# Two attention stages rearranged: search, sums and division in one, the latent heads moved to the other

## The chip, the cores and the metric

The program runs on one core of one Trainium2 chip. It computes one mixture-of-experts block and two layers of a second network on 1024 tokens of width 1024, all in fp32. The metric is the device time of one execution in microseconds (us), lower is better.

## The reference, cut to what matters

Three kinds of dense attention are touched: the latent heads of the first block, and in each of the two layers of the second block the "map" heads and the "grouped" heads. All are a plain softmax over all keys:

```python
# first block, latent heads: 8 heads, q and k of 96 (64 + 32 rotary), v of 64, 1024 queries, 1024 keys
s = jnp.einsum('bqhd,bkhd->bhqk', q_blk, k).astype(jnp.float32) * scale
p = jax.nn.softmax(s, axis=-1).astype(v.dtype)
return jnp.einsum('bhqk,bkhd->bqhd', p, v)

# second block, two layers: 1024 + 256 context keys
# map heads: 4 heads x 2 maps = 8 softmaxes of width 32, v of 64
s = jnp.einsum('bqhmd,bkhmd->bhmqk', q, k).astype(jnp.float32) * (q.shape[-1] ** -0.5)
p = jax.nn.softmax(s, axis=-1)
a = (p[:, :, 0] - lam * p[:, :, 1]).astype(v.dtype)
# grouped heads: 6 query heads of 64 on 2 key heads
```

Layer 0 of the second block also attends from the 256 context queries to the 256 context keys. Layer 1 does not need them.

## The kernel before, in words

The program is a sequence of stages. In each, every engine has its own instruction stream written out in a loop, and semaphores order them. Where a stage ends, all engines meet. The stages of this change, by the prefix of their buffers: `am` (latent heads), `ad` (dilated heads, not changed, but it uses the function that `am` moves to), then per layer `aa` (map heads), `ab` (grouped heads) and `ac` (near heads, not changed).

**`stage_turned`** (L1193) puts keys on the partitions. Heads go in pairs. Per pair there are blocks of queries, `(q0, qn, k0, k1)`: two of 512 queries, and in layer 0 a third of 256 context queries. A step `g` is one tile of 128 keys of one block: 8 steps a block in `am`, 10 in `aa` and `ab`, 2 in the small block. In a step TensorE computes the scores of both heads into one half of `sp_` (`scores`), ScalarE takes the exponential into `pT`, a ring of RP = 6. On odd steps TensorE multiplies two steps of `pT` with v into `po` (`values`). The denominators are sums over keys. VectorE adds some steps of `pT` into `accd`, GpSimd the others into `accp` (`on_dve` says which), VectorE adds the two, TensorE sums over the partitions with a matrix of ones (`sums`), and VectorE takes the reciprocal of the 128x512 result and multiplies `po` with it (`normalised`). TensorE turns the product, and ScalarE copies it (`finished`).

The maximum that the exponential subtracts must be known before a block starts, as a row added to the query operand. It comes from a search: TensorE computes cheaper scores with queries on the partitions, in pieces of up to 512 keys, into one of the two banks of `mp`, and VectorE takes the maximum of each. `searched(g)` lists the pieces done in step `g`, for blocks ahead. `search` waits in TensorE until the piece two before it is reduced (`mc`). `row_at(B)` is the step after which the maxima are turned, copied by ScalarE, written to HBM and read back as the row; the block's first `scores` waits for that (`rw`). Piece 0 to len-1 of the first block are searched before any step.

In a step VectorE does its `search` pieces, then `add(g - 2)`, then `normalised`, in that order, and TensorE does `scores`, the search pieces, then (odd steps) `sums` and `values`, then `turned`, `row`.

**`stage_attention`** (L884) puts queries on the partitions. A step `h` is one tile of 128 queries of one head, with all its keys (1024: two banks of one of SB = 3 PSUM buffers). TensorE computes scores(h), VectorE takes the maximum, ScalarE the exponential with its sum in two halves, TensorE turns the probabilities of step h - 2 back into the same PSUM buffer, and they are copied out: in `ad` by ScalarE alone (`by_act`), and where there is no `add_bias`, the first half by ScalarE and the second by VectorE (`by_dve`, `turned_part`). VectorE does that copy after the maximum of step h, and scores(h + 1) waits for it:

```python
                        if h >= SB:
                            pe.wait_ge(eva, it * n + (h - LAG))
                            pe.wait_ge(evd, it * n + (h - LAG))
```

The pairs of heads go in a hardware loop of 2 rounds with 2 pairs each.

Of the kernel before, what the change touches and what calls it, by code (L numbers as in the profile page):

```python
# [133 lines left out]
def _build(nc, a, k, out, ctx):  # L134
# [1058 lines left out]
    def stage_turned(name, dq, pairs, nq, sk, blocks, aside=None):  # L1193
# [39 lines left out]
        def searched(g):  # L1233

            p, B, blk, i = where(g)
            if size[blk] <= 2:
                return []
            ahead = [B + 1] if blk + 1 < NB and size[blk + 1] > 2 else [b for b in (B + 1, B + 2) if b % NB == 0 or size[b % NB] <= 2]
            if blk == 0 and NB == 3:
                ahead = [B + 1, B + 2]  # L1240
            if blk == 1 and NB == 3:
                ahead = [B + 2]
# [10 lines left out]
        out_at = {end(B) + F_AT: B for B in range(NBLK)}  # L1253

        def items(g):

            return (g in out_at) + (rows_at.count(g) if g >= 0 else 0)
# [7 lines left out]
        def slot_out(B):  # L1265
            g = end(B) + F_AT
            return before[g] + (g < TOT)

        def slot_row(B):
            g = rows_at[B]  # L1270
            return 0 if B == 0 else before[g] + (g < TOT) + (g in out_at) + rows_at[:B].count(g)

        pieces_before = [len(maxima(0))]
        for g in range(TOT + 10):
            pieces_before.append(pieces_before[-1] + (len(searched(g)) if g < TOT else 0) +
                                 any(end(B) + D_AT == g for B in range(NBLK)))

        def slot_den(B):
            return pieces_before[end(B) + D_AT + 1] - 1


        def on_dve(blk, i):
            return size[blk] <= 2 or i in (0, 1, size[blk] - 1)
# [11 lines left out]
        with ExitStack() as st_:  # L1295
# [10 lines left out]
            rB, oT, o = sb("rB", [P, 512]), sb("oT", [P, 2, 512]), sb("o", [P, 2, 4, 2 * dv])  # L1306
# [76 lines left out]
            def _(pe):  # L1383
# [48 lines left out]
                def sums(B):  # L1432
# [20 lines left out]
                for g in range(TOT + F_AT):  # L1453
# [1243 lines left out]
```

## Time and profile before

| | us |
|---|---|
| median of 3 runs | 5038.33 (5033.85 to 5042.69) |
| the profiled execution, its own time | 5035.54 |
| its span in the profile | 5033.9 |

| engine | busy us | share of the span |
|---|---|---|
| PE (TensorE matmul) | 3815.4 | 76% |
| PEld (weight load) | 2694.3 | 54% |
| DVE (VectorE) | 2606.4 | 52% |
| ACT (ScalarE) | 1773.2 | 35% |
| POOL (GpSimd) | 1407.2 | 28% |

Shares are means over stages with different limits. In a timeline row stand the start, the busy time, engine, line and operation, output and inputs, how many instructions are merged, and in brackets the idle time before them with what ended it ("DVEq L1111" is VectorE's queue at that line). A `PEclk` of 1.0 is the full TensorE clock of 2.4 GHz, 0.5 is 1.2 GHz.

### The profile page before, as it was taken

Reading aid. Unit: us, or ns where it says so; the run is one execution under the profiler, and the core shown is the slowest. Engines: PE = TensorE matmul, PEld = TensorE weight load, DVE = VectorE, ACT = ScalarE, POOL = GpSimd, SP = SyncE. Lnnn points to the kernel's source line nnn. Section 1 sums busy time; section 2 is a strip of 40 time slices with the busy share of each in tenths; the row PEclk is TensorE's granted clock in tenths of the full one; section 3 lists DMA queues with packets and bytes.
Section 4 is the critical chain, followed back from the end, with each engine's and each line's share of the span. In section 5 each row is a group of like instructions: output and inputs, shape, how many; then the busy total and the mean of one; then the engine's idle time right before and its main releaser. Section 6 shows DMA issues by size and latency. Waiting matters only on the chain. (4 is left out here: it accounts for less than half of the span.)

```text
span 5033.9 us, 55601 instructions
## 1 busy us (share of the span) xinstructions
PE 3815.4 (76%) x18714; PEld 2694.3 (54%) x18714; DVE 2606.4 (52%) x4549; ACT 1773.2 (35%) x2670; POOL 1407.2 (28%) x974
## 2 busy tenths in 40 slices
PE   3985886886299995589968868576688978858557
PEld 3973444665278884477833334355576753324346
DVE  2114453432678786744445546466556535545465
ACT  1225224731077774422212312354422212312352
POOL 0213231000056662144613413200044613423102
PEclk6997798997699997799967868888799977868798
DMA  5228213316699994322232032423222331131333
GB/s 210 97 107 243 66 38 72 102 47 237 167 396 398 394 394 175 102 88 92 97 90 52 9 77 47 92 82 109 81 97 76 102 78 59 26 71 40 88 105 90
DMA packets 327678, 628.00 MB, mean 125 GB/s; under 512 B 115338, under 2 KB 171892, under 8 KB 326364
## 3 DMA queue, kind: packets, MB, share of 16 engines
q1 hardware_dynamic: 289080, 494.92, 31.4%
q0 software_dynamic: 34240, 113.67, 7.1%
q10 hardware_dynamic: 4068, 15.79, 0.8%
q8 instruction: 152, 2.49, 0.2%
q14 instruction: 138, 1.13, 0.1%
HBM read 485.18 MB, written 139.11 MB: 124 GB/s over the span
## 5 line engine op out<-in xcount | busy, mean ns | idle before, releaser
L2282 PE MATMUL pr_ps<-pr_wH,hT_part 128*128 128x512 f32 x1120 | 447.5, 400 | 0.0
L2052 ACT ACTIVATE ex_high<-ex_ring 128x2048 fp32r<-128x2048 f32 x192 | 368.7, 1920 | 96.0 <-PE ex_pg L2028 37.6
L2098 DVE TENSOR_TENSOR ex_ring_part<-ex_ring,ex_high 128x2048 fp32r<-128x2048 f32 x144 | 371.8, 2582 | 50.7 <-ACTq L2053 38.8
L2282 PE MATMUL pr_ps<-pr_wH,x_sb_part 128*128 128x512 f32 x896 | 366.2, 409 | 22.8 <-DVEq L2355 22.8
L2282 PE MATMUL pr_ps<-pr_w_part,x_sb_part 128*128 128x512 f32 x896 | 358.9, 401 | 0.0
L1519 DVE TENSOR_REDUCE aa_part<-aa_mp 128x1 f32<-128x512 f32 (+1 forms) x400 | 238.1, 595 | 207.1 <-PE aa_mp L1396 171.8
L1993 POOL TENSOR_TENSOR ex_ring_part<-ex_ring,ex_high 128x2048 fp32r<-128x2048 f32 x48 | 239.4, 4988 | 215.3 <-ACTq L2053 215.3
L1396 PE MATMUL aa_mp<-aa_kA,aa_qA 96*128 96x512 f32 (+1 forms) x400 | 199.0, 538 | 120.9 <-DVEq L1520 73.7
L1487 ACT ACTIVATE aa_pT<-aa_sp 128x1024 f32<-128x1024 f32 (+1 forms) x168 | 168.6, 1003 | 313.1 <-PE aa_sp L1417 304.1
L1519 DVE TENSOR_REDUCE ab_part<-ab_mp 128x1 f32<-128x512 f32 (+1 forms) x300 | 178.7, 596 | 182.8 <-PE ab_mp L1396 155.6
L2282 PEld LDWEIGHTS pr_ps<-pr_wH,hT_part 128*128 128x128 f32 x1120 | 217.2, 194 | 47.5
L2428 POOL TENSOR_TENSOR pr_w_part<-pr_w,pr_wH 128x512 fp32r<-128x512 f32 x96 | 124.4, 1296 | 406.8 <-ACTq L2308 405.2
L1396 PE MATMUL ab_mp<-ab_kA,ab_qA 128*128 128x512 f32 (+1 forms) x300 | 141.9, 515 | 120.1 <-DMA ab_v<-proj 57.1
L1658 PE MATMUL o_ps<-o_wH,o_yT 128*128 128x512 f32 x832 | 231.5, 396 | 0.0
L1587 POOL TENSOR_TENSOR aa_accp<-aa_accp,aa_pT 128x1024 f32<-128x1024 f32 x80 | 194.3, 2429 | 94.0 <-ACTq L1488 91.1
L1487 ACT ACTIVATE ab_pT<-ab_sp 128x1024 f32<-128x1024 f32 (+1 forms) x126 | 126.4, 1003 | 255.2 <-PE ab_sp L1417 250.8
L1396 PEld LDWEIGHTS aa_mp<-aa_kA,aa_qA 96*128 96x128 f32 x400 | 94.0, 236 | 226.2 <-DVEq L1520 170.5
L1428 PE MATMUL aa_po<-aa_pT,aa_v 128*64 128x512 f32 x672 | 213.2, 769 | 0.0
L2282 PEld LDWEIGHTS pr_ps<-pr_wH,x_sb_part 128*128 128x128 f32 x896 | 175.3, 196 | 58.5 <-issue 23.4
L2368 DVE TENSOR_REDUCE pr_ss<-pr_sqr 128x8 f32<-128x512 f32 (+2 forms) x80 | 49.6, 619 | 287.8 <-ACTq L2331 284.1
L1045 PE MATMUL ac_ps<-ac_kT,ac_qT 128*128 128x384 f32 (+1 forms) x204 | 75.4, 374 | 155.8 <-DVEq L1111 84.2
L2282 PEld LDWEIGHTS pr_ps<-pr_w_part,x_sb_part 128*128 128x128 f32 x896 | 174.7, 195 | 34.9
(387 smaller groups left out, 9026.5 us busy)
## 6 DMA issues: line engine op xcount, KB each, us to landing
ex_ring<-in_w_gate SPq DMA_DIRECT2D x64, 1024.0 KB, 9.6
ex_ring<-in_w_up SPq DMA_DIRECT2D x64, 1024.0 KB, 8.1
ex_ring<-in_w_down SPq DMA_DIRECT2D x64, 1024.0 KB, 7.9
z_d<-pr_zT POOLq DMA_DIRECT2D x120, 256.0 KB, 3.0
rt_mw<-in_w_ada SPq DMA_DIRECT2D x14, 2048.0 KB, 15.6
pr_w<-in_w_in SPq DMA_DIRECT2D x14, 2048.0 KB, 8.5
mod_w<-in_w_ada SPq DMA_DIRECT2D x10, 2048.0 KB, 13.1
proj<-pr_raw POOLq DMA_DIRECT2D x60, 256.0 KB, 2.3
```

The costliest lines, as they stand in the source:

```text
L1045: mm = tensor.matmul(ps[h % SB][:, at:at + m], q.bitcast(F32R), kk.bitcast(F32R), start=i == 0, stop=i == len(ab) - 1)
L1396: tensor.matmul(mp[:, k_ % 2, 0:w], qA[rows, b, j, q0:q0 + P].bitcast(F32R), kA[rows, b, j, a_:a_ + w].bitcast(F32R), start=True, stop=Tru ...
L1428: mm = tensor.matmul(po[j * dv:(j + 1) * dv, B % 2, 0:qn], v[:, p % 2, k0 // P + i, j * dv:(j + 1) * dv], pT[:, g % RP, j, 0:qn], start=i ...
L1487: scalar.activation(pT[:, g % RP, :, 0:qn], sp_[:, s % 2, :, 0:qn], ACT.Exp)
L1519: vector.tensor_reduce(part[:, B % 2, j * n + t, x:x + 1], mp[:, k_ % 2, 0:w], AX.X, ALU.max)
L1587: pool.tensor_tensor(acc, pT[:, (g - 3) % RP, :, 0:qn] if i == 3 else acc, pT[:, (g - 2) % RP, :, 0:qn], ALU.add).then_inc(ap_, 1)
L1658: mm = tensor.matmul(ps[:, t % 2, cols], yT[:, t % 2, part, c, :].bitcast(F32R), w[:, c, cols].bitcast(F32R), start=c == 0 and i == 0, sto ...
L1993: pool.tensor_tensor(w_part[:, c % SL].bitcast(F32R), w_sb[:, c % SL], wH[:, c % HL], ALU.subtract)\
L2052: scalar.activation(wH[:, c % HL].bitcast(F32R), w_sb[:, c % SL], ACT.Copy)
L2098: vector.tensor_tensor(w_part[:, c % SL].bitcast(F32R), w_sb[:, c % SL], wH[:, c % HL], ALU.subtract)
L2282: mm = tensor.matmul(ps[:, g % 4, :], x.bitcast(F32R), w[:, c % 2, kk, :].bitcast(F32R), start=kk == 0 and i == 0, stop=kk == KC - 1 and i ...
L2428: pool.tensor_tensor(w_part[w].bitcast(F32R), w_sb[w], wH[w], ALU.subtract).then_inc(w_low, 1)
```

## The change: the diff

Stage `am` goes from `stage_turned` to `stage_attention`. In `stage_turned` the search pieces are spread evenly over all but the last two steps of a block (3 or 3.5 a step instead of 4), their row is sent one step after the last of them, not two; all adds but the first go to GpSimd; VectorE's adds move from step g - 2 to g - 3. The sums over partitions are computed with queries on the partitions, one column a head and tile. ScalarE copies `po` as it is, TensorE turns it into `mp`, and VectorE multiplies the turned output with the small reciprocals.

```diff
-            ahead = [B + 1] if blk + 1 < NB and size[blk + 1] > 2 else [b for b in (B + 1, B + 2) if b % NB == 0 or size[b % NB] <= 2]
...
+            ahead = [B + 1] if NB == 2 else [B + 1, B + 2] if blk == 0 else [B + 2]
             pcs = [(b, m) for b in ahead if b < NBLK for m in range(len(maxima(b)))]
-            return pcs[4 * i:4 * i + 4]
+            n = size[blk] - 2
+            return pcs[-(-len(pcs) * i // n):-(-len(pcs) * (i + 1) // n)] if i < n else []
...
-            return 2 + max(g for g in range(TOT) if any(b == B for b, _ in searched(g)))
+            return 1 + max(g for g in range(TOT) if any(b == B for b, _ in searched(g)))
...
-        D_AT, F_AT, S_AT = 4, 6, 8
+        O_AT, D_AT, F_AT, S_AT = 3, 4, 6, 8
...
-            return size[blk] <= 2 or i in (0, 1, size[blk] - 1)
+            return i < 2
...
                 def sums(B):
...
-                    for j in range(2):
-                        mm = tensor.matmul(mp[j * dv:(j + 1) * dv, k_ % 2, 0:qn], ones[:, j * dv:(j + 1) * dv],
-                                           accd[:, B % 2, j, 0:qn], start=True, stop=True)
+                    for t in range(qn // P):
+                        for j in range(2):
+                            mm = tensor.matmul(mp[:, k_ % 2, 2 * t + j:2 * t + j + 1], accd[:, B % 2, j, t * P:(t + 1) * P],
+                                               ones[:, 0:1], start=True, stop=True)
                     mm.then_inc(mf, 1)
 
                 def turned(B):
-                    s = slot_out(B)
+                    k_ = slot_out(B)
                     pe.wait_ge(nr, B + 1)
-                    pe.wait_ge(sr, s - 1)
+                    pe.wait_ge(mc, k_ - 1)
                     for t in range(tiles_of(B)):
-                        mm = tensor.transpose(sp_[:, s % 2, 0, t * P:(t + 1) * P], oT[:, B % 2, t * P:(t + 1) * P], ident[:, :])
-                    mm.then_inc(st, 1)
+                        mm = tensor.transpose(mp[:, k_ % 2, t * P:(t + 1) * P], oT[:, B % 2, t * P:(t + 1) * P], ident[:, :])
+                    mm.then_inc(mf, 1)
...
+                    for B in range(NBLK):
+                        if end(B) + D_AT == g:
+                            sums(B)
+                    for B in range(NBLK):
+                        if end(B) + F_AT == g:
+                            turned(B)
                     if g % 2:
...
                         for x in (g - 3, g - 2):
                             if 0 <= x < TOT:
                                 values(x)
-                    if g in out_at:
-                        turned(out_at[g])
...
-                def finished(B):
...
+                def gathered(B):
+                    qn = blocks[B % NB][1]
+                    act.wait_ge(pv, end(B) + 1)
                     if B >= 2:
...
+                        act.wait_ge(mf, slot_out(B - 2) + 1)
+                    scalar.activation(oT[:, B % 2, 0:qn], po[:, B % 2, 0:qn], ACT.Copy)
+                    act.drain().then_inc(nr, 1)
...
+                    for B in range(NBLK):
+                        if end(B) + O_AT == g:
+                            gathered(B)
...
                 def add(g):
                     p, B, blk, i = where(g)
                     qn, n = blocks[blk][1], size[blk]
+                    if i == n - 1 and n > 2:
+                        last = added(g)
+                        dve.wait_ge(*last)
+                        vector.tensor_tensor(accd[:, B % 2, :, 0:qn], accd[:, B % 2, :, 0:qn], accp[:, B % 2, :, 0:qn], ALU.add)
+                        dve.drain().then_inc(ac, 1)
...
-                def normalised(B):
-                    qn, k_ = blocks[B % NB][1], slot_den(B)
+                def sums(B):
+                    n, k_ = 2 * tiles_of(B), slot_den(B)
                     dve.wait_ge(mf, k_ + 1)
-                    vector.reciprocal(rB[:, 0:qn], mp[:, k_ % 2, 0:qn])
+                    vector.reciprocal(rd[:, B % 2, 0:n], mp[:, k_ % 2, 0:n])
                     dve.drain().then_inc(mc, 1)
...
-                    vector.tensor_tensor(oT[:, B % 2, 0:qn], po[:, B % 2, 0:qn], rB[:, 0:qn], ALU.mult)
...
+                def divided(B):
+                    n, k_ = 2 * tiles_of(B), slot_out(B)
+                    dve.wait_ge(mf, k_ + 1)
                     if B >= 2:
+                        dve.wait_ge(os_[B % 2], 16 * (B // 2))
+                    vector.tensor_tensor(o[:, B % 2, 0:n // 2, :].rearrange("p t (j d) -> p (t j) d", d=dv),
+                                         mp[:, k_ % 2, 0:n * dv].rearrange("p (c d) -> p c d", d=dv),
+                                         rd[:, B % 2, 0:n].rearrange("p (c o) -> p c o", o=1).to_broadcast([P, n, dv]), ALU.mult)
+                    dve.drain().then_inc(mc, 1)
...
-                    if 0 <= g - 2 < TOT:
-                        add(g - 2)
+                    if 0 <= g - 3 < TOT:
+                        add(g - 3)
...
-        stage_turned("am", QD, [mla(p // 2, p % 2) for p in range(H1 // 2)], S, S, [(0, 512, 0, S), (512, 512, 0, S)])
+        stage_attention("am", 2, 2, mla, QD, S, every)
```

## Rows read from the trace of the kernel before

**Rows 1.** Windows: us, PE, PEld, DVE, ACT, POOL busy, PEclk, DMA share, GB/s

```profile
4206.00:4319.00 113.00, 96.67 (x280) 38.03 (x279) 67.09 (x90) 33.30 (x36) 44.51 (x22) 0.80 0.23 51
4552.00:4665.00 113.00, 96.79 (x331) 46.09 (x331) 67.08 (x90) 32.27 (x35) 42.27 (x21) 0.88 0.21 45
```

**Rows 2.** Timeline, first and last work of stage am

```profile
507.33 1.19 PE L1396 MATMUL am_mp<-am_kA,am_qA 96*128 96x512 f32 x2 [35.75 <-DMA am_v<-v_mla]
...
787.95 0.77 POOL L1593 DMA_DIRECT2D att<-am_o  x1 [10.04 <-ACTq L1496]
```

**Rows 3.** Timeline of stage ad: starts of steps, a late step, its end

```profile
814.88 0.79 PE L1045 MATMUL ad_ps<-ad_kT,ad_qT 128*128 128x512 f32 x1 [27.88 <-DMA ad_v<-proj]
...
823.19 0.50 PE L1045 MATMUL ad_ps<-ad_kT,ad_qT 128*128 128x512 f32 x1 [2.30 <-ACTq L1161]
...
918.75 0.50 PE L1045 MATMUL ad_ps<-ad_kT,ad_qT 128*128 128x512 f32 x1
...
1041.31 0.50 PE L1045 MATMUL ad_ps<-ad_kT,ad_qT 128*128 128x512 f32 x1
...
1042.34 1.03 PE L1055 MATMUL ad_ps<-ident,ad_prob 128*128 128x128 f32 x8
1042.69 1.23 DVE L2566 CUSTOM_DVE_ANT_0 ad_ps<-ad_ps,logc 128x1024 f32<-128x1024 f32 x1 [1.11 <-PE ad_ps L1045]
...
1043.30 1.09 PE L1071 MATMUL ad_po<-ad_pT,ad_v 128*64 128x128 f32 x16
...
1055.05 0.89 POOL L1187 DMA_DIRECT2D att<-ad_o  x1 [46.24 <-DVEq L1130]
```

**Rows 4.** VectorE groups, shapes apart: busy us, mean ns, idle before and releaser

```profile
L1519 DVE TENSOR_REDUCE aa_part<-aa_mp 128x1 f32<-128x512 f32 x256 | 177.0, 691 | 173.9 <-PE aa_mp L1396 153.6
L1110 DVE COPY ac_pT<-ac_ps 128x256 f32<-128x256 f32 x96 | 40.7, 424 | 13.1 <-issue 1.4 <-PE ac_ps L1055 0.9
```

**Rows 5.** Timeline of stage ac: VectorE's copy and the scores that wait for it

```profile
3260.29 0.42 DVE L1110 COPY ac_pT<-ac_ps 128x256 f32<-128x256 f32 x1
...
3260.89 0.41 PE L1045 MATMUL ac_ps<-ac_kT,ac_qT 128*128 128x384 f32 x1 [0.71 <-DVEq L1111]
```

**Rows 6.** Timeline of one block of stage ab in layer 1

```profile
4588.32 0.50 PE L1417 MATMUL ab_sp<-ab_qA,ab_kA 128*128 128x512 f32 x1
...
4589.81 2.85 DVE L1519 TENSOR_REDUCE ab_part<-ab_mp 128x1 f32<-128x512 f32 x4 [10.42 <-PE ab_mp L1396]
...
4594.85 1.94 PE L1428 MATMUL ab_po<-ab_pT,ab_v 128*64 128x512 f32 x8
...
4596.71 0.51 PE L1417 MATMUL ab_sp<-ab_qA,ab_kA 128*128 128x512 f32 x1
...
4604.58 1.98 PE L1437 MATMUL ab_mp<-ab_accd,ab_one 128*64 128x512 f32 x4
...
4606.84 3.36 DVE L1546 RECIPROCAL ab_rB<-ab_mp 128x512 f32<-128x512 f32 x1
4608.79 0.50 PE L1417 MATMUL ab_sp<-ab_qA,ab_kA 128*128 128x512 f32 x1
...
4625.96 0.50 PE L1417 MATMUL ab_sp<-ab_qA,ab_kA 128*128 128x512 f32 x1
```

**Rows 7.** Timeline of stage aa in layer 1: a row's way, and two block starts

```profile
4277.78 0.27 ACT L1478 ACTIVATE aa_nmT<-aa_sp 8x128 fp32r<-8x128 f32 x1 [0.51 <-PE aa_sp L1404]
...
4281.31 0.73 PE L1417 MATMUL aa_sp<-aa_qA,aa_kA 97*128 97x512 f32 x2 [0.59 <-DMA aa_qA<-aa_nmd]
...
4318.72 0.73 PE L1417 MATMUL aa_sp<-aa_qA,aa_kA 97*128 97x512 f32 x2 [0.43 <-DMA aa_qA<-aa_nmd]
```

**Rows 8.** Costliest groups of the page: busy us, mean ns, idle before and releaser

```profile
L1587 POOL TENSOR_TENSOR aa_accp<-aa_accp,aa_pT 128x1024 f32<-128x1024 f32 x80 | 194.3, 2429 | 94.0 <-ACTq L1488 91.1
```

**Rows 9.** Timeline of the end of stage ab in layer 1

```profile
4683.07 8.12 POOL L1587 TENSOR_TENSOR ab_accp<-ab_accp,ab_pT 128x1024 f32<-128x1024 f32 x3
...
4700.55 0.77 POOL L1593 DMA_DIRECT2D att<-ab_o  x1 [9.37 <-ACTq L1496]
```

More of the change, by code:

```diff
@@ L1249, in row_at @@
                 return -1
-            return 2 + max(g for g in range(TOT) if any(b == B for b, _ in searched(g)))
+            return 1 + max(g for g in range(TOT) if any(b == B for b, _ in searched(g)))
         rows_at = [row_at(B) for B in range(NBLK)]
-        D_AT, F_AT, S_AT = 4, 6, 8
-        out_at = {end(B) + F_AT: B for B in range(NBLK)}
+        O_AT, D_AT, F_AT, S_AT = 3, 4, 6, 8
         def items(g):
-            return (g in out_at) + (rows_at.count(g) if g >= 0 else 0)
+            return rows_at.count(g) if g >= 0 else 0
         before = [1]
@@ L1263, in slot_scores @@
             return before[g]
[L1265 to L1267 removed]
         def slot_row(B):
             g = rows_at[B]
[L1271 removed]
+            return 0 if B == 0 else before[g] + (g < TOT) + rows_at[:B].count(g)
         pieces_before = [len(maxima(0))]
@@ L1275, in stage_turned, with slot_out @@
             pieces_before.append(pieces_before[-1] + (len(searched(g)) if g < TOT else 0) +
-                                 any(end(B) + D_AT == g for B in range(NBLK)))
+                                 sum(end(B) + D_AT == g for B in range(NBLK)) + sum(end(B) + F_AT == g for B in range(NBLK)))
         def slot_den(B):
-            return pieces_before[end(B) + D_AT + 1] - 1
+            return pieces_before[end(B) + D_AT + 1] - 1 - any(end(b) + F_AT == end(B) + D_AT for b in range(NBLK))
+        def slot_out(B):
+            return pieces_before[end(B) + F_AT + 1] - 1
         def on_dve(blk, i):
-            return size[blk] <= 2 or i in (0, 1, size[blk] - 1)
+            return i < 2
         dve_adds = [sum(on_dve(b, i) and i > 0 for b, i in steps[:s]) for s in range(NSTEP + 1)]
@@ L1452, in _ @@
                 row(0)
-                for g in range(TOT + F_AT):
+                for g in range(TOT + F_AT + 1):
                     if g < TOT:
@@ L1457, in _ @@
                             search(B, m, pieces_before[g] + x)
+                    for B in range(NBLK):
[4 more added lines that the diff above has]
+                            turned(B)
                     if g % 2:
-                        for B in range(NBLK):
-                            if end(B) + D_AT == g:
-                                sums(B)
                         for x in (g - 3, g - 2):
@@ L1563, in _ @@
                     search(0, m, m)
-                for g in range(TOT + F_AT):
+                for g in range(TOT + F_AT + 1):
                     if g < TOT:
@@ L1567, in _ @@
                             search(B, m, pieces_before[g] + x)
-                    if 0 <= g - 2 < TOT:
-                        add(g - 2)
+                    if 0 <= g - 3 < TOT:
+                        add(g - 3)
                     for B in range(NBLK):
                         if end(B) + D_AT == g:
-                            normalised(B)
+                            sums(B)
+                    for B in range(NBLK):
+                        if end(B) + F_AT == g:
+                            divided(B)
             @block.gpsimd
```

25 lines of the change are left out of this document (4 added, 21 removed).

## The prediction

> **What bounds the kernel now.** I looked at windows over the touched stages, then their timelines, to see at each step who waits. No engine is full: in two steady stretches of 113 us, VectorE is busy 67 us, and TensorE shows 97 us of overlapping records at a granted clock of 0.80 in `aa` and 0.88 in `ab` [rows 1]. So the price of a block is a chain, and I read one block of `ab` step by step [rows 6]. Two steps (even, odd) make a round, since `values` comes on odd steps. The block takes 4625.96 - 4588.32 = 37.6 us: first round 8.4, second 12.1 (4596.71 to 4608.79, with `sums` and the reciprocal of 3.36), the other three 17.2. The search sets the early rounds: a piece goes to TensorE only when the piece two before it is reduced, and a reduction of 512 takes 0.69 [rows 4]. The late rounds hold almost no search and are short. `am` has the same shape. It lasts from 507.33 to 787.95, 280.6 us [rows 2].
>
> **Part 1, the latent heads.** The trace has the function they move to at work on as many heads, queries and keys: `ad` runs from 814.88 to 1055.05, 240.2 us, and 28 of its steps take 918.75 - 823.19 = 95.6, or 3.41 each [rows 3]. Three things differ. A step has 6 score matmuls of 512 columns instead of 4; ScalarE copies half of the turned probabilities; VectorE copies the other half, and the next scores wait for it. I follow that chain from the first score matmul. In `ad` VectorE's maximum starts 1042.69 - 1041.31 = 1.38 later [rows 3]; two more matmuls at 0.23 (eight of 512 columns take 1.94 in `values`, the last end included, [rows 6]) make 1.84. The maximum over 1024: 424 ns for 256 and 691 for 512 [rows 4] give 1.04 ns an element, so 1.23, which the 128x1024 operation in `ad` also takes [rows 3]. A gap of 0.12, then the copy of 512 from PSUM, 0.69 by the same slope. In `ac` the copy ends at 3260.71 and the waiting scores start at 3260.89 [rows 5], 0.18. Sum 4.06 a step. TensorE itself has less: scores 1.50, transposes 0.97, values 1.03 [rows 3], with the turned output every second step about 3.65 on the mean. So the chain decides, and 56 steps cost 56 x (4.06 - 3.41) = 36.4 more than in `ad`; the start and end of each round of the loop add 0.4 each. 240.2 + 36.4 + 0.8 = 277.4 against 280.6: -3.2, of which the last store, now of eight tiles instead of four, takes back some 0.5. I take -3. Bounds: if the copy hid altogether, 3.65 a step would give -23 more; a longer gap of the loop's dynamic addresses +5.
>
> **Part 2, a searched block of `ab`, layer 1.** Prices as in rows 4 and 6: scores of a step 0.95, a search matmul 0.23, first reduction 0.43 after it, then one each 0.81 (512) or 0.54 (256), `values` 1.94. Every step now has three pieces (512, 512, 256).
> - A plain round: pieces 1 and 2 go at 1.05 and 1.28, reductions end at 2.17, 2.98 and 3.52; scores of the odd step 2.40 to 3.35, piece 4 at 3.4, piece 5 at 3.7; piece 6 must wait for reduction 4, at 4.6; `values` 4.75 to 6.6. The same walk with 4 + 4 pieces gives 8.5 where the trace has 8.4. So round 1 gains 1.8.
> - Round 2. At step g = end + 3, an even one, VectorE adds `accd` and `accp` (1.23 + 0.12) between reductions 3 and 4. Before, its adds fell on odd steps, behind the last reduction, while TensorE ran `values`. Now reduction 4 ends at 5.7, piece 6 goes at 5.8, `sums` waits for reduction 5 at 6.6. `sums` itself: 16 small instructions with 128 weight columns. Bounds: 16 x 0.064 (1.03 for 16 with 64 weight columns) = 1.0 and 16 x 0.121 (0.97 for 8 transposes with 128) = 1.9 [rows 3]; I take 1.5. `values` then ends at 10.2. Before 12.1: gain 1.9. The reciprocal of 8 columns costs nothing, since it runs beside `values`.
> - Rounds 3 to 5, before 17.2. Round 3: the add of step 1 also falls on an even step, and `turned` now waits for a bank of `mp`: 9.05. Round 4 is a plain one, 6.6. Round 5: the row is sent after step 8 instead of 7. It needs ScalarE, which first does the exponential of step 8 (1.02, till 2.2), and then 4281.31 - 4277.78 = 3.53 to the scores of the next block [rows 7]: 5.9. Sum 21.6, a loss of 4.4.
>
> Net +0.7 a block. GpSimd's seventh add is no bound: 7 x 2.43 = 17 us in a block of 38 [rows 8]; ScalarE loses one copy (`finished`) and gains one of the same size. Cover: if GpSimd's last add came after 3.6 us of round 2, VectorE would wait in front of all reductions of that block.
>
> **Part 3, the others.** `ab` has 5 such blocks in layer 1: +4. `aa` in layer 1 has 7, and its scores are half as long: the same walk gives 35.6 at the full clock, and for the kernel before 34, where the trace shows 4318.72 - 4281.31 = 37.4 [rows 7]. The 3.4 between is what the low clock costs there (granted 0.80, [rows 1]); I carry it over: 39.0, so +1.6 a block, +11. In layer 0 the small block lies between the row and its use or the row comes at the same step as before, so the loss of round 5 is absent: about -1.4 a block in `ab` (5 blocks, -7), and -0.5 in `aa` (7 blocks, -4), where 28 pieces a block instead of 24 leave less to spread. Ends of the four stages: before, the last three adds of GpSimd end at 4691.2, then come 1.23 + sums + 3.36 + 0.69 + transposes + copy, and the store at 4700.55 [rows 9]. After: one more add of 2.4, less 0.8 since no VectorE add slows the others (8.12 for three against 3 x 2.43, [rows 8]), the addition 1.3, sums 2.1, transposes 0.9, division 0.8: 4698.2 or so for the store, -2.3. With a small block at the end (layer 0) two long reciprocals go: -3.3. Together -11.
>
> **Sum.** -3 + 4 + 11 - 7 - 4 - 11 = -10 us. The profiled execution took 5035.5, so 5025.5; the median stands 2.8 higher: **5028**. That is 0.2% faster, just what a measurement of this kernel can tell from no change (0.2%, 10 us). Unknown sizes: `am` -23 to +5, `sums` 24 blocks x (-0.5 to +0.4) = -12 to +10.
>
> The Trainium skill prices the weights of `sums` (TensorE: Matmul & The Clock Gate, "LDWEIGHTS (loading the stationary operand)"): columns / 1.2 ns, 107 ns for 128. An estimate by that page: 16 x 0.107 = 1.7, which would put the sum at -5 in place of -10. No run here shows such a matmul with one moving column.
>
> **Rivals.**
> - *The clock falls in every block (slower).* Round 2 and 3 of a new block have a hole: from 3.9 to 6.6 TensorE issues one piece or none. And the dense late rounds, which ran at the full clock (1.94 for two `values` steps), are gone. If TensorE goes down to 1.2 GHz behind both holes, each pair of `values` takes about 3.5 instead of 1.94. Place: 24 blocks x 2; price 3.2 a block, less what the clock takes already (0.9 in `ab`, so 2.3 more on 10 blocks; in `aa` 1.5 more on 14): +44, in all +34, 5072. It decides from the seventh lost pair on (7 x 1.6 = 11). For: 0.80 in `aa` already. Against: in [rows 6] TensorE is nearly idle for some 2.5 us behind the reciprocal and goes on at 0.23 a matmul.
> - *The clock stays up (faster).* Even rounds without search bursts keep TensorE more evenly busy; then `aa` gets back its 3.4 in 14 blocks: -48 more, 4980.
> - *`am` is bound by TensorE alone (faster)*, the copy hidden: 3.65 a step, 5005. Against: in `ac` the copy is shown as what ends the wait [rows 5].
> - *Nothing is gained by the spread and nothing lost*: search and row trade evenly in all blocks, leaving -3 - 11 and the division, within 0.2%.
>
> The Trainium skill has a rule for the first rival (same page, "A second HAM failure mode: psum-queue depth-cycling"): matmul groups with small idle gaps, cycling through PSUM banks, make the clock go up and down. By that rule the small gaps of the new rounds would be enough. Rows 1 agree for the kernel before (0.80 and 0.88).
>
> **How the numbers follow.** Forecast 0.36, falling clock 0.29, steady clock 0.17, fast `am` 0.12, even trade 0.06. The forecast sits on the edge: 0.20 of it counts as faster, 0.13 as within 0.2%, 0.03 as slower. Faster: 0.20 + 0.17 + 0.08 = 0.45 with two thirds of the fast `am`; slower 0.03 + 0.27 = 0.30; within 0.2% the rest, 0.25. The forecast's own range with its unknown sizes is 5010 to 5042. The range of 8 in 10 reaches to the cases on both sides: 4988 to 5070.
>
> **What would show it.** `am`: 4.06 a step between first score matmuls, with the wait ended by VectorE's queue at L1111; 3.65 would show the copy hidden. A searched block of `ab` in layer 1 of 38.4 us with plain rounds of 6.6, a second round near 10, and a DMA wait of 1 to 2 us in front of each next block. `sums` 1.0 to 1.9. `PEclk` of `aa` in layer 1 near 0.80; below 0.7 the first rival holds, above 0.9 the second. Wrong altogether it would be if VectorE's add did not delay the reductions behind it.

## The result, and the profile after

| | before | after |
|---|---|---|
| median, same chip, 4 runs each | 5036.09 us (5030.64 to 5042.69) | 5165.8 us (5155.92 to 5171.21) |
| span of the profiled execution | 5033.9 | 5169.6 |
| granted TensorE clock, mean | 0.851 | 0.847 |

The ratio is 1.0255, with a 95% interval of 1.0234 to 1.0276: 2.5% slower. The forecast was 5028, with a range of 4988 to 5070; it missed by 138 us and by its sign.

Where the time went, by stage. `am` is taken from its first matmul to its last store, the other four from their first exponential to the start of their last row of stores (where that row holds two stores 0.7 us apart, as in layer 0 of the kernel after, the first counts, so sums of four stages can be short by 1.4):

| stage | before | after | forecast of the difference | measured |
|---|---|---|---|---|
| `am` | 280.6 | 267.0 | -3 | -13.7 |
| `aa`, layer 0 | 318.5 | 360.7 | -4 | +42 |
| `ab`, layer 0 | 243.6 | 276.1 | -7 | +33 |
| `aa`, layer 1 | 297.2 | 335.6 | +11 | +38 |
| `ab`, layer 1 | 221.9 | 252.4 | +4 | +31 |

(The forecast had -11 more for the four stage ends.) So everything that was lost lies in `stage_turned`, about evenly over its 24 blocks that search for another: 5.5 to 6.6 us each by stage. From here on "the turned stages" are these four together: 1081 us before, 1225 after.

The timeline of the kernel after, one block of `ab` in layer 1 (start, duration, engine, line, operation, output and inputs, idle time before it and what ended that). It answers to [rows 6]:

```profile
4712.16 0.50 PE L1413 MATMUL ab_sp<-ab_qA,ab_kA 128*128 128x512 f32 x1 [0.49 <-DMA ab_qB<-ab_nmd]
...
4718.97 0.50 PE L1413 MATMUL ab_sp<-ab_qA,ab_kA 128*128 128x512 f32 x1
...
4722.61 1.23 DVE L1533 TENSOR_TENSOR ab_accd<-ab_accd,ab_accp 128x1024 f32<-128x1024 f32 x1
...
4724.73 0.39 PE L1392 MATMUL ab_mp<-ab_kA,ab_qA 128*128 128x256 f32 x1 [1.66 <-DVEq L1519]
4725.63 3.03 PE L1434 MATMUL ab_mp<-ab_one,ab_accd 128*128 128x1 f32 x16 [0.51 <-DVEq L1519]
4728.59 3.68 PE L1424 MATMUL ab_po<-ab_pT,ab_v 128*64 128x512 f32 x8
...
4732.20 0.80 PE L1413 MATMUL ab_sp<-ab_qA,ab_kA 128*128 128x512 f32 x1
...
4734.98 5.66 POOL L1596 TENSOR_TENSOR ab_accp<-ab_accp,ab_pT 128x1024 f32<-128x1024 f32 x2 [8.86 <-ACTq L1486]
...
4736.19 2.25 DVE L1539 TENSOR_TENSOR ab_accd<-ab_pT 128x1024 f32<-128x1024 f32 x1
...
4739.33 0.39 PE L1392 MATMUL ab_mp<-ab_kA,ab_qA 128*128 128x256 f32 x1 [2.68 <-DVEq L1519]
...
4741.24 2.92 PE L1424 MATMUL ab_po<-ab_pT,ab_v 128*64 128x512 f32 x8
...
4744.09 0.50 PE L1413 MATMUL ab_sp<-ab_qA,ab_kA 128*128 128x512 f32 x1
...
4750.90 0.50 PE L1413 MATMUL ab_sp<-ab_qA,ab_kA 128*128 128x512 f32 x1
...
4756.88 0.50 PE L1413 MATMUL ab_sp<-ab_qA,ab_kA 128*128 128x512 f32 x1 [0.55 <-DMA ab_qB<-ab_nmd]
```

Read the starts of scores: rounds of 6.8, 13.2, 11.9, 6.8 and 6.0 us, 44.7 in all. Before they were 8.4, 12.1, 9.3, 4.0 and 3.9, 37.6 ([rows 6], which leave out the starts of its rounds 4 and 5, scores at 4618.07 and 4622.04).

In rounds 2 and 3 an addition of VectorE stands between reductions, TensorE sits idle for 1.66 and 2.68 us in front of the third piece, and behind each hole of this block its matmuls run at about half speed: `values` takes 3.68 and 2.92 instead of 1.94. The addition beside GpSimd takes 2.25 instead of 1.23. In all four stages TensorE's idle times in the timelines add up to 246 us; in the kernel with only the heads moved (m below) they are 179. So 67 us of the loss are waits, and the rest is longer work.

One step of `am` in the kernel after, and the start of the next:

```profile
591.06 1.62 PE L1045 MATMUL am_ps<-am_kT,am_qT 96*128 96x512 f32 x6 [0.35 <-DVEq L1111]
...
592.72 1.23 DVE L1139 TENSOR_REDUCE am_nm<-am_ps 128x1 f32<-128x1024 f32 x1 [1.84 <-PE am_ps L1045]
...
594.06 0.69 DVE L1110 COPY am_pT<-am_ps 128x512 f32<-128x512 f32 x1
...
594.93 1.61 PE L1045 MATMUL am_ps<-am_kT,am_qT 96*128 96x512 f32 x6 [0.24 <-DVEq L1111]
```

The wait is ended by VectorE's copy, as foreseen, but a step takes 594.93 - 591.06 = 3.87, not 4.06. The maximum starts 1.66 behind the first score matmul instead of 1.84.

Granted clock of the turned stages in the kernel after (window, us, busy PE, PEld, DVE, ACT, POOL, PEclk, DMA share, GB/s):

```profile
2568.00:2929.00 361.00, 290.12 (x922) 138.33 (x920) 147.02 (x239) 95.90 (x111) 147.21 (x67) 0.74 0.13 36
2986.00:3262.00 276.00, 226.43 (x815) 123.28 (x814) 106.05 (x172) 71.87 (x83) 108.64 (x49) 0.82 0.10 23
4196.00:4531.00 335.00, 257.81 (x812) 116.34 (x811) 135.76 (x207) 88.03 (x95) 145.93 (x63) 0.79 0.13 36
4583.00:4835.00 252.00, 198.41 (x722) 104.09 (x720) 98.14 (x149) 66.34 (x71) 108.20 (x47) 0.87 0.10 23
```

The same stages in the kernel before:

```profile
2578.00:2896.00 318.00, 260.90 (x809) 107.47 (x807) 185.21 (x247) 95.72 (x111) 125.16 (x59) 0.78 0.15 41
2952.00:3195.00 243.00, 202.24 (x730) 99.86 (x728) 138.90 (x179) 71.61 (x83) 91.91 (x44) 0.87 0.12 26
4129.00:4427.00 298.00, 247.28 (x718) 97.38 (x717) 164.66 (x215) 88.53 (x95) 120.76 (x56) 0.78 0.15 41
4479.00:4701.00 222.00, 187.36 (x649) 89.96 (x647) 122.35 (x155) 65.95 (x71) 90.20 (x42) 0.87 0.11 26
```

VectorE's busy time over the four fell from 611 to 487 us (the long reciprocals went), and the stages still grew. The mean clock tells little in layer 1 (0.79 and 0.87 against 0.78 and 0.87); in layer 0 it fell from 0.78 and 0.87 to 0.74 and 0.82. What it hides is when the clock is low: in the block above while `sums` and `values` run. In the block of [rows 6] it was low too, over search pieces, the old `sums` (1.98 there, 1.08 in other blocks) and part of `values`, but those lost less: 0.9 by `sums`, 0.6 by `values` (2.52).

### The profile page after: what moved, and what is told of

It reads as the page before. It is cut to its first block and busy times, and to the rows that moved or that the text cites. A ratio compares the mean times of both kernels' runs of the same rounds, so it can differ in the third digit from the quotient of the medians.

```text
span 5169.6 us, 59446 instructions
## 1 busy us (share of the span) xinstructions
PE 3890.5 (75%) x20190; PEld 2848.3 (55%) x20190; DVE 2477.1 (48%) x4568; ACT 1848.7 (36%) x2943; POOL 1414.9 (27%) x966
## 5 line engine op out<-in xcount | busy, mean ns | idle before, releaser
L1392 PE MATMUL aa_mp<-aa_kA,aa_qA 96*128 96x512 f32 (+1 forms) x400 | 185.6, 500 | 150.2 <-DVEq L1519 108.8
L1596 POOL TENSOR_TENSOR aa_accp<-aa_accp,aa_pT 128x1024 f32<-128x1024 f32 x96 | 238.5, 2484 | 191.9 <-ACTq L1486 188.1
L1392 PE MATMUL ab_mp<-ab_kA,ab_qA 128*128 128x512 f32 (+1 forms) x300 | 127.2, 480 | 140.1 <-DVEq L1519 81.1
L1424 PE MATMUL aa_po<-aa_pT,aa_v 128*64 128x512 f32 x672 | 224.3, 805 | 0.0
L1596 POOL TENSOR_TENSOR ab_accp<-ab_accp,ab_pT 128x1024 f32<-128x1024 f32 x72 | 177.9, 2471 | 139.4 <-ACTq L1486 136.6
```

Of the source, the lines that this page charges most:

```text
L1392: tensor.matmul(mp[:, k_ % 2, 0:w], qA[rows, b, j, q0:q0 + P].bitcast(F32R), kA[rows, b, j, a_:a_ + w].bitcast(F32R), start=True, stop=Tru ...
L1424: mm = tensor.matmul(po[j * dv:(j + 1) * dv, B % 2, 0:qn], v[:, p % 2, k0 // P + i, j * dv:(j + 1) * dv], pT[:, g % RP, j, 0:qn], start=i ...
L1596: pool.tensor_tensor(acc, pT[:, (g - 3) % RP, :, 0:qn] if i == 3 else acc, pT[:, (g - 2) % RP, :, 0:qn], ALU.add).then_inc(ap_, 1)
```

## The experiments

All ratios are against the kernel before on the same chip. "Turned" is the sum of the four stages in the profile.

| kernel | median us | ratio, 95% interval | turned |
|---|---|---|---|
| m: heads moved, nothing else | 5031.3 | 0.9985 (0.9971 to 0.9999) | 1084 |
| ms: m + spread search, late row | 5041.6 | 1.0009 (1.0000 to 1.0019) | 1099 |
| ms7: m + spread over 7 steps, row as before | 5023.3 | 0.9965 (0.9954 to 0.9977) | 1083 |
| mv: m + division on the turned output | 5076.1 | 1.0073 (1.0056 to 1.0089) | 1123 |
| mva: mv + additions as after | 5158.7 | 1.0233 (1.0216 to 1.0250) | 1219 |
| mv_late: mv + additions one step later only | 5199.0 | 1.0309 (1.0285 to 1.0332) | 1257 |
| mva_sums6: mva + sums two steps later | 5132.3 | 1.0182 (1.0163 to 1.0200) | 1195 |
| mv_seven: mva_sums6 + VectorE's additions on odd steps | 5041.1 | 1.0006 (0.9994 to 1.0018) | 1110 |
| msv_seven: the same + spread search | 5063.4 | 1.0044 (1.0030 to 1.0058) | 1117 |
| mv_seven_r: mv_seven + one-pass sums | 4995.9 | 0.9919 (0.9902 to 0.9935) | 1045 |
| m_fill: m + 2 idle matmuls a piece | 5001.9 | 0.9930 (0.9913 to 0.9946) | 1057 |
| m_fill4: m + 4 | 5128.1 | 1.0172 (1.0155 to 1.0189) | 1190 |
| after_fill: after + 2 | 5090.5 | 1.0109 (1.0088 to 1.0129) | 1150 |
| mv_seven_r_fill: mv_seven_r + 2 | 4903.1 | 0.9729 (0.9713 to 0.9745) | 964 |
| mv_seven_r_fill_s7: the same + search as in ms7 | 4905.3 | 0.9741 (0.9725 to 0.9758) | 961 |

**One part at a time.** Theory 1 was that TensorE's clock falls behind holes made by the additions and the sums; theory 2 that the spread itself, which takes the dense late rounds away, costs most; theory 3 that the sums do. The filled kernels put idle matmuls of 512 columns on TensorE in front of each search piece but a step's first.

m changes one line of the kernel before:

```
-        stage_turned("am", QD, [mla(p // 2, p % 2) for p in range(H1 // 2)], S, S, [(0, 512, 0, S), (512, 512, 0, S)])
+        stage_attention("am", 2, 2, mla, QD, S, every)
```

> The kernel before with the latent heads moved to stage_attention and nothing else. Both theories: the traces give am 280.6 us before and 267.0 after, so this kernel stands 14 us below the kernel before (about 5022), and its four turned stages (two aa, two ab) last as before: 343.8, 269.7, 297.2 and 221.9 us. If the time of the turned stages differed by more than 3 us each, the move itself would have a price elsewhere.

`am` took 266.5 us, 14 less, and the turned stages 1084, 3 more (`aa` +3.5 in layer 0 and -3.2 in layer 1; the expectation's 343.8 and 269.7 count layer 0 from its first search, the table from the first exponential). The profiled executions differ by 10 (5025.3 against 5035.5), the medians by 6, with 1 to 15 inside the interval. Stages that are the same in all kernels move by some us from one execution to the next: the first search of `aa` in layer 0 starts between 2533 and 2546 us in the kernels with `am` moved. So for single parts the turned stages say more than the medians, though they come from one execution each; both are given where they differ.

ms adds `searched` and `row_at` of the change:

```
+            n = size[blk] - 2
+            return pcs[-(-len(pcs) * i // n):-(-len(pcs) * (i + 1) // n)] if i < n else []
...
-            return 2 + max(g for g in range(TOT) if any(b == B for b, _ in searched(g)))
+            return 1 + max(g for g in range(TOT) if any(b == B for b, _ in searched(g)))
```

> The latent heads moved, and of the edits in stage_turned the spread search with the row one step later, nothing else (division on [dims, queries], additions as before). Theory 1 (TensorE's clock falls behind holes; the holes come from the additions on even steps and from the sums): without those the three-piece rounds are plain, about 6.6 us in ab layer 1, and only the late row costs: a block 37.6 - 1.8 + 4.4 - 2 = 38 us, the whole kernel within 15 us of the one with the heads alone. Theory 2 (the spread itself takes the dense late rounds away, and with them the full clock): the turned stages lose some 60 us or more of the 144 us that were lost, granted clock of ab layer 1 at 0.85 or below, of aa layer 1 at 0.76 or below.

10 us over m, 15 in the turned stages. Theory 2 falls: the spread alone is not where 130 us went.

mv is m with the new `sums`, `turned`, `gathered` and `divided`, but with `searched`, `row_at`, `on_dve` and `add` of before.

> The latent heads moved, and of the edits in stage_turned only the division on the turned output (sums with the queries on the partitions, reciprocal of 8 columns, ScalarE gathers, turned goes to mp); search, row and additions as in the kernel before. Theory 1 (holes from the additions on even steps and from late sums): here the reductions are done by step 6, the reciprocal of 3.36 us is gone, the sums take 1.5 to 3 us, so each of 24 blocks gains 0 to 2 us and the kernel is 0 to 45 us faster than the one with the heads alone. Theory 3 (the 16 small matmuls with 128 weight columns cost 3 us at the low clock and bring the clock down): each block loses 1 us or more, 25 us in all, and values behind the sums run at 3 us or more.

45 us over m, 39 in the turned stages: theory 3 holds for this part. TensorE waits less (its idle times in the timelines of the four stages add up to 147 us against 179), but `sums` takes 3.54 us in most blocks, where the old ones took 1.98 [rows 6] or 1.08.

mva is the change with the old search (and the old `ahead` and row):

```
...
-            n = size[blk] - 2
+            return pcs[4 * i:4 * i + 4]
...
```

> The latent heads moved and all edits in stage_turned but the spread: the search stands at four pieces a step again and the row goes one step after the last but one as before; the division on the turned output and the additions of the kernel after (seventh addition on GpSimd, VectorE's one step later, on even steps). Theory 1 (additions on even steps between reductions make the holes): with four reductions a step the additions hold up even more, and most of the loss stays: at least 70 of the 144 us in the turned stages. Theory 2 (the spread takes away the dense late rounds): most of the loss is gone, the kernel is within 40 us of the one with the heads alone.

83 us over mv, 96 in the turned stages: the additions are the largest part. TensorE's waits for reductions grew from 116 us in mv to 162, so about half of it is waiting; the rest is longer work.

**Which property of the additions.** The edit to them has two: VectorE's come one step later, which makes it an even one, and the last step of a block goes to GpSimd.

mv_late moves only the time:

```
-                    if 0 <= g - 2 < TOT:
-                        add(g - 2)
+                    if 0 <= g - 3 < TOT:
+                        add(g - 3)
```

> The kernel with the latent heads and the division moved (its turned stages last 1123 us together from the first exponential of each to its last store, against 1219 with the additions of the kernel after), and of the edit to the additions only its time: VectorE does each of its additions one step later, on even steps, the last step is still added by VectorE. Theory A1 (the even step is the harm: an addition of 1.23 us stands before reductions that TensorE's pieces wait for): most of the 96 us, at least 60. Theory A2 (the seventh addition on GpSimd is the harm: VectorE waits for it in front of reductions, and its own operations slow down beside GpSimd): under 30 us.

It is the slowest of all, 123 us over mv (waits for reductions: 219 us). The timeline of mv_late in a block of `ab` shows the queue: two additions in a row, the second at 3.23 beside GpSimd, TensorE idle for 5.01 in front of its next piece, then everything slow:

```profile
4698.38 1.23 DVE L1537 TENSOR_TENSOR ab_accd<-ab_accd,ab_pT 128x1024 f32<-128x1024 f32 x1
4699.54 2.34 POOL L1597 TENSOR_TENSOR ab_accp<-ab_pT 128x1024 f32<-128x1024 f32 x1 [11.79 <-ACTq L1489]
4699.72 3.23 DVE L1542 TENSOR_TENSOR ab_accd<-ab_accd,ab_accp 128x1024 f32<-128x1024 f32 x1
4703.85 0.58 PE L1395 MATMUL ab_mp<-ab_kA,ab_qA 128*128 128x256 f32 x1 [5.01 <-DVEq L1522]
...
4705.29 3.55 PE L1437 MATMUL ab_mp<-ab_one,ab_accd 128*128 128x1 f32 x16
4708.77 3.68 PE L1427 MATMUL ab_po<-ab_pT,ab_v 128*64 128x512 f32 x8
```

mv_seven keeps GpSimd's seventh addition and mends the times:

```
-        O_AT, D_AT, F_AT, S_AT = 3, 4, 6, 8
+        O_AT, D_AT, F_AT, S_AT = 3, 6, 6, 8
...
-                    if 0 <= g - 3 < TOT:
-                        add(g - 3)
+                    if 0 <= g - 4 < TOT:
+                        joined(g - 4)      # accd + accp, taken out of add
...                                            # sums(B)
+                    if 0 <= g - 2 < TOT:
+                        add(g - 2)
```

> The same base, with the seventh addition on GpSimd but no addition of VectorE on an even step of the search: the first one two steps behind its exponential as before, the joining of the two accumulators four steps behind (an odd step, behind that step's reductions), the sums two steps later. Theory A1: the 96 us are gone but for 10 or so (TensorE waits under 1.5 us a block more for reductions than in the base). Theory A2: 60 us or more stay.

117 us under mva, 35 under mv (109 and 13 in the turned stages); TensorE waits 110 us for reductions. In its timeline the two additions lie beside `values` and beside the scores, and the reductions behind them are not late:

```profile
4570.09 2.85 DVE L1521 TENSOR_REDUCE ab_part<-ab_mp 128x1 f32<-128x512 f32 x4 [0.33 <-PE ab_mp L1395]
...
4572.10 1.94 PE L1427 MATMUL ab_po<-ab_pT,ab_v 128*64 128x512 f32 x8
4573.06 1.43 DVE L1547 TENSOR_TENSOR ab_accd<-ab_accd,ab_accp 128x1024 f32<-128x1024 f32 x1
4574.61 1.23 DVE L1537 TENSOR_TENSOR ab_accd<-ab_pT 128x1024 f32<-128x1024 f32 x1
4575.95 2.85 DVE L1521 TENSOR_REDUCE ab_part<-ab_mp 128x1 f32<-128x512 f32 x4
```

This kernel moved the sums too, so mva_sums6 moves only them (`D_AT` 6 in mva):

> The kernel with the heads, the division and the additions of the kernel after and the old search (5159), with one edit: the sums come six steps behind the end of a block instead of four; VectorE's additions stay on even steps. The kernel with both mended stands at 5041. If the place of the additions is the cause, the loss against 5041 stays: above 5110. If the sums two steps behind their accumulator are (they close the chain joining, sums, values), it falls below 5075.

26 us of the 117 come from the later sums, 91 from the new times of the additions (24 and 85 in the turned stages). One of them moved earlier and the other later, and both now fall on odd steps; in mv_late a move the other way, from odd to even, cost 123. So it is the parity and not the delay as such, though an odd step at another distance was not run. The seventh addition costs nothing that can be seen: mv_seven has it and is not slower than mv.

msv_seven is the whole change with the mended times.

> All of the change, with only the times of VectorE's additions mended (first addition two steps behind, joining four steps behind, on odd steps; sums two steps later). If the even-step additions alone made the loss, this stands by the kernel with the same mended additions and no spread (1110 us in the turned stages, 5041 in all) plus what the spread costs on its own, 15 us: 5050 to 5060, and TensorE's waits for reductions fall from 175 us in the kernel after to under 130. If the spread search needs the additions elsewhere too (its steps have no gap behind the reductions), it stays above 5085.

5063 is 3 above the first expectation and 102 under the kernel after: the times of the additions and sums alone give back three quarters of the loss or a little more. TensorE's waits for reductions fall from 190 us in the kernel after to 121 (the expectation counted 175 and asked for under 130). What the spread costs here is known only roughly: 22 by the medians, 6 by the turned stages.

ms7 spreads over seven steps (`n = size[blk] - 3`), which leaves the row at its old step.

> The latent heads moved, and the search spread over seven steps of ten instead of eight, so that the row is sent behind the same step as in the kernel before. The spread over eight cost 10 us against the heads alone. If the late row costs that (DMA wait in front of a block, exponential before it), this is 5 to 20 us faster than the spread over eight and at or below the heads alone (5031). If the lost dense rounds cost it, it stays at 5036 or above.

18 us under ms (16 in the turned stages): that is the late row. TensorE waited 24 us for ScalarE's exponentials in ms and 0.3 here. Against m it is level in the turned stages and 8 us faster by the medians: the spread without the late row costs nothing and brings little.

**The clock.** m_fill puts work that nobody needs where TensorE would wait for a reduction; it is written into the half of `sp_` that the next scores overwrite (and waits for the exponential that still reads that half):

```
...
+                    if s is not None:            # every piece but a step's first
+                        pe.wait_ge(sr, s)
+                        for _ in range(2):
+                            tensor.matmul(sp_[:, (s + 1) % 2, 0, 0:512], qA[rows, b, j, q0:q0 + P].bitcast(F32R),
+                                          kA[rows, b, j, 0:512].bitcast(F32R), start=True, stop=True)
                     if k_ >= 2:
                         pe.wait_ge(mc, k_ - 1)
```

> The kernel with only the latent heads moved, plus two idle matmuls of 512 columns (their output is overwritten unread) on TensorE in front of every search piece but a step's first, that is where TensorE waits for a reduction. They do none of the kernel's work. Theory 1 (the clock falls behind the waits and this is what costs): granted clock in the four turned stages rises from 0.78 to 0.88 to 0.95 or more, pairs of values fall from a mean of 2.3 to below 2.1, time 20 to 60 us less, less the delays by the filling. Theory 2 (the chain of reductions alone sets the time): no gain, or a loss of up to 50 us since each filling can delay a piece by 0.2.

> The kernel after, with the same idle matmuls in the same places. Theory 1: more than half of the loss of 144 us in the turned stages comes back, since sums go from 3.5 to 1.8 and pairs of values from 2.4-2.8 to 1.94. Theory 2: the additions between reductions and the late row keep their cost, at least 73 us of waits stay, and the time falls by under 70 us.

Both gain, m 29 us and the kernel after 75. The windows of `aa` and `ab` in layer 1, first of m:

```profile
4119.00:4413.00 294.00, 242.21 (x717) 95.00 (x715) 164.65 (x215) 88.31 (x95) 120.56 (x56) 0.80 0.15 41
4467.00:4690.00 223.00, 187.38 (x649) 89.91 (x647) 122.54 (x155) 65.97 (x71) 89.69 (x41) 0.87 0.11 25
```

then of m_fill:

```profile
4099.00:4392.00 293.00, 257.58 (x968) 138.71 (x967) 164.66 (x215) 88.16 (x95) 120.82 (x55) 0.90 0.15 42
4445.00:4662.00 217.00, 199.88 (x830) 115.65 (x829) 123.19 (x155) 66.49 (x71) 89.94 (x42) 0.96 0.12 26
```

PEclk rises by 0.1, in `aa` to 0.90 and not to the 0.95 that was expected. And `aa` in layer 1 gained nothing from it: 294.0 us in m and 293.5 in m_fill, with most blocks at 37.5 in both. The 27 us came from the other three stages. Whether the filling took there what the clock gave was not told apart. after_fill shows the price of the clock best, since two of its blocks of `ab` in layer 1 run the same instructions with and without it. The one that starts its exponentials at 4587.94 takes 45.0 us, the next 40.2. TensorE's sums and values in the first, then in the second:

```profile
4600.29 3.02 PE L1439 MATMUL ab_mp<-ab_one,ab_accd 128*128 128x1 f32 x16 [0.52 <-DVEq L1524]
4603.24 3.68 PE L1429 MATMUL ab_po<-ab_pT,ab_v 128*64 128x512 f32 x8
...
4645.24 1.92 PE L1439 MATMUL ab_mp<-ab_one,ab_accd 128*128 128x1 f32 x16 [0.52 <-DVEq L1524]
4647.09 1.94 PE L1429 MATMUL ab_po<-ab_pT,ab_v 128*64 128x512 f32 x8
...
4655.76 0.39 PE L1397 MATMUL ab_mp<-ab_kA,ab_qA 128*128 128x256 f32 x1 [1.77 <-DVEq L1524]
...
4657.22 1.94 PE L1429 MATMUL ab_po<-ab_pT,ab_v 128*64 128x512 f32 x8
```

Rounds 2 and 3 (from the exponentials) are 13.6 and 11.6 in the first, 10.4 and 10.1 in the second. TensorE's waits in front of these rows agree within 0.03 in the two blocks, in both rounds; what sent the clock down in one and not in the other is not shown. With the filling in both, the change still costs 1150 - 1057 = 93 us of the 141 that it costs without. So the filling gives back about 48 of what the change cost. The clock's part may be larger, since after_fill still has granted clocks of 0.87 to 0.93 over the four stages, but the filling has a price of its own that was not measured. Neither theory alone was enough.

> The kernel with the latent heads alone moved and four idle matmuls in each place instead of two. They take 0.93 us at the full clock, longer than the 0.58 that TensorE would wait for a reduction of 512. Clock theory: no more is to be had in ab (clock 0.96 to 0.98 with two), so this is slower than with two by 0.2 to 0.4 us for each of some 500 pieces, 50 us or more; aa (clock 0.90) may gain 10. If the filling worked by something else than the clock (an effect of order or of waits), four would work as well as two.

126 us over m_fill, in `aa` too, where a gain of 10 was thought possible. The clock is up (0.95 to 0.99 over the four stages), but four idle matmuls take 0.93 us, longer than a hole of 0.58. So it is not "more is better".

**The sums.** mv_seven_r writes the joined sum, rounded to fp32r, into a buffer of its own, and feeds TensorE with that (two equal columns of ones, every second result used):

```
-                            mm = tensor.matmul(mp[:, k_ % 2, 2 * t + j:2 * t + j + 1], accd[:, B % 2, j, t * P:(t + 1) * P],
-                                               ones[:, 0:1], start=True, stop=True)
+                            mm = tensor.matmul(mp[:, k_ % 2, 4 * t + 2 * j:4 * t + 2 * j + 2], accr[:, B % 2, j, t * P:(t + 1) * P].bitcast(F32R),
+                                               onesr[:, 0:2].bitcast(F32R), start=True, stop=True)
```

> The kernel with mended additions and no spread, with the accumulator of the sums rounded to fp32r into a buffer of its own, so that the small matmuls of the sums are one pass each: 8 instead of 16 in a block of 512 queries. Theory 3 (the sums cost TensorE 3.5 us at the low clock and 1.8 to 1.9 at the full one, against 2.0 and 1.1 before, about 50 us over 24 blocks): with half as many, the sums take 1.8 and 0.9, so 24 to 45 us come back: 4996 to 5017. Rival (TensorE has slack there, the chain of reductions sets the pace, since the sums now lie two steps behind): under 10 us.

```profile
4527.75 1.02 PE L1438 MATMUL ab_mp<-ab_oner,ab_accr 128*128 128x2 f32 x8 [0.52 <-DVEq L1523]
```

45 us by the medians, the upper end; 65 in the turned stages, but that execution was 18 under its kernel's median. The new buffer also frees `accd` earlier, which was not told apart.

> The same with the two idle matmuls in front of every search piece but the first of a step. The filling gave 32 us on the kernel with the heads alone and 75 on the kernel after. If its gain is that of the clock, it gives 25 to 40 us here too: 4960 to 4990, the fastest of all. If the shorter sums have already brought the clock back, it gives nothing.

93 us (81 in the turned stages), more than twice what was expected: the gains are not a sum. The four turned stages have a clock of 0.97 to 0.98, and blocks of `ab` in layer 1 that took 37.4 to 41.3 in mv_seven take 35.5 each:

```profile
4052.00:4311.00 259.00, 237.01 (x1001) 132.73 (x999) 129.38 (x207) 88.49 (x95) 138.64 (x64) 0.97 0.17 47
4363.00:4568.00 205.00, 196.04 (x854) 119.91 (x852) 94.24 (x149) 66.53 (x71) 103.96 (x48) 0.98 0.13 28
```

At 4903.1 this is the fastest kernel, 2.7% under before (0.9729, 0.9713 to 0.9745).

> The fastest kernel so far (division, mended additions, one-pass sums, two idle matmuls a piece: 4903) with the search over seven steps and the row at its old step. If three to four pieces a step leave VectorE and TensorE fewer bursts to wait in, it gains 5 to 25 us. If the rounds are bound by TensorE now (idle matmuls included), nothing changes, since it issues the same instructions: 4895 to 4910.

No gain: the old search does as well once the clock is held.

## Why the prediction was wrong

**`am` (-3, measured -14).** The mechanism was right, the chain through VectorE's copy. Only the first term, scores to maximum, was 1.66 instead of 1.84; over 64 steps that is the 11 us.

**Rounds 1, 4 and 5 of a searched block (6.6, 6.6, 5.9; measured 6.8, 6.8, 6.0).** Right, with the DMA wait ahead of the next block where it was foreseen. ms7 confirms the cause of the last: without the late row 16 to 18 us come back.

**Round 2 (10.2; measured 13.2) and round 3 (9.05; measured 11.9).** This is the step that failed. The order of events was right: piece 3 waits, sums behind it, then values. With the clock up it takes 10.4 and 10.1 (after_fill), within 0.2 and 1.1 of the walk. But the walk used prices of the full clock for work that stands right behind a hole. In round 2 `sums` took 3.03 instead of 1.5, and `values` 3.68 instead of 1.94, together 3.3 more. In round 3 the addition took 2.25 instead of 1.23, `values` 2.92 instead of 1.94, the transposes 1.09 instead of 0.63, and the scores lost 0.3, together 2.8. The two rounds took 25.1 where the walk has 19.25; the block of after_fill at the full clock took 20.5. So, by these two blocks, 4.6 of the missing 5.9 go with the low clock, and 1.3 with prices that were too low at any clock: `sums` and the addition beside GpSimd. If all 24 blocks missed 5.9, that would be 140, about what the forecast missed in all.

**`sums` 1.0 to 1.9.** At the full clock 1.84 to 1.92, the upper bound and the row of the transposes. At the low clock 3.54, for which the range had no place. One-pass sums gave back 45 us. The estimate from the Trainium skill (TensorE: Matmul & The Clock Gate, "LDWEIGHTS (loading the stationary operand)") was 1.7, nearer to the 1.84 of the full clock than the 1.5 taken.

**The clock carried over.** The forecast kept the 3.4 us a block that `aa` lost before. `aa` blocks in layer 1 went from 37.5 to 44.3, where 1.6 more was expected. That these 3.4 are the low clock's price was argued and is not borne out: in m_fill the clock of that stage is 0.90 and most of its blocks still take 37.5. The rival "the clock falls in every block" had the mechanism, the place, and nearly the size of what filling gives back: 44 against 48. What it lacked is that its other terms, the additions between reductions at their true price, were wrong as well. The evidence held against it (TensorE going on fast after an idle 2.5 us behind the reciprocal) came from one block, and that same block ran its `sums` at the low clock. The sign set for it was no help either: `PEclk` of `aa` in layer 1 came out at 0.79, near the 0.80 of the forecast, since the mean hides where the clock is low. The rule of the Trainium skill that was named with this rival (TensorE: Matmul & The Clock Gate, "A second HAM failure mode: psum-queue depth-cycling") fits what the filling showed: small gaps and a low clock, and nearly the full clock once they are filled.

**Layer 0 (-7 and -4; measured +33 and +42).** The same rounds 2 and 3 are there; that the small block lies ahead of the row's use could not repay them.

**The addition on an even step.** The forecast counted 1.3 us of delay to a reduction and took it as hidden by the shorter rounds. Both additions on even steps cost 91 us, 3.8 a block: the delay, the hole, and the low clock that follows. GpSimd's seventh addition was rightly taken as harmless.

**Stage ends (-11).** The last block of `ab` in layer 1, from its first exponential to the last store, took 33.0 before and 32.9 after, where -2.3 was expected: the last `sums` ran at 3.58. In layer 0 the small block at the end took 18.7 instead of 17.0 in `aa` and 16.0 instead of 13.8 in `ab`, where -3.3 was expected.

## What to carry to other kernels

When a chain is walked from a trace, price the work that stands behind a hole at both clocks, and look where the low clock would fall, not at its mean. On an engine that releases another's buffers, an operation of 1.2 us can cost next to nothing in the step where the other has work of its own, and more than its own length in the step where it does not (two of them cost 3.8 us a block here); test the parity of a schedule before its content. Where holes of half a microsecond can't be removed, filling them with just as much idle TensorE work can pay (0.6% on m, 1.5% on the kernel after, 1.9% on mv_seven_r), and twice as much cost m 1.9%.

## What the runs showed of the hardware

- An fp32 matmul with one moving column and 128 weight columns is two instructions of 0.12 us at the full clock and 0.22 at the low one (16 in 1.84 and 3.54). Eight transposes with 128 moving and 128 weight columns take the same 0.12 each (0.97), 16 matmuls with 64 weight columns half of that (1.03), by the working in the prediction: in these rows the time goes with the weight columns. In fp32r each matmul is one instruction (8 in 1.02, with two moving columns).
- An addition of VectorE over 128x1024 in SBUF takes 1.23 us alone, and 2.25, 3.16 or 3.23 beside one of GpSimd. In the kernel after and in mv_late each of the 69 that began while one of GpSimd ran ended 1.1 us behind it (in mv_late above 4702.95 against 4701.88), and each of GpSimd's that began while one of VectorE ran ended 2.2 or 2.3 behind that. It looks as if the two took turns.
- The same block of the same kernel took 45.0 and 40.2 us within one execution, with equal waits in front of the sums (0.52) and TensorE at one or the other clock behind them (`sums` 3.02 and 1.92, `values` 3.68 and 1.94).
